# A two-layer hybrid step on one core: the attention stage's instruction order rewritten on every engine, and a second and third place for the output projection in PSUM

## The chip, the cores and the metric

The kernel runs on one core of a Trainium2 chip. The metric is the device time of one execution in microseconds (us), the median of three runs: 1716.8 us (1716.34 to 1719.81). Engines are named as in the profile: PE (matrix multiply) with its weight loads PEld, DVE (vector), ACT (activation), POOL (GpSimd), SP (the queue that issues the transfers).

## The reference, cut to what matters

Two layers act on 1024 prompt tokens and 64 sample tokens. Each layer projects the normed input, runs a gated recurrence (branch A), a top-k attention (branch B, 4 heads) and a differential attention (branch C, 4 heads with two softmax maps each), concatenates the three, projects with `w_out`, norms, and adds to the input. All of the change lies in the attention and output-projection part:

```python
def dsa_block(...):                                   # branch B
    s = einsum('bqhd,bqkhd->bqhk', q, k_sel) * (B_HEAD_DIM ** -0.5)
    p = softmax(where(valid, s, -inf))
    return einsum('bqhk,bqkhd->bqhd', p, v_sel)
def diff_block(...):                                  # branch C
    s = einsum('bqhid,bkhid->bhiqk', q, k) * (C_HALF ** -0.5)
    p = softmax(where(mask, s, -inf), axis=-1)
    attn = p[:, :, 0] - lam * p[:, :, 1]
    return rmsnorm(einsum('bhqk,bkhe->bqhe', attn, v), subln) * (1.0 - lam_init)
...
    mix = einsum('ble,ed->bld', concatenate([y_a, y_b, y_c], axis=-1), p['w_out'])
    x = x + rmsnorm(mix, p['norm_post'])
```

## The kernel before, in words

A layer has a front (input projections, index scores, top-k by bisection, recurrence), which the change doesn't touch, and then the **attention stage**. There are nine tiles of query tokens, taken in `ORDER` = 7, sample, 6, 0, 1, 2, 3, 4, 5; tile t < 8 has 128 tokens and sees 128(t+1) keys, the sample has 64 tokens and 1088 keys. `ATT` (L100) lists 70 **units**, one per tile, branch and head: first the four C heads, then the B heads of a tile (the sample's B heads are taken two at a time). "Wide" below means more than 512 keys (tiles 7, 6, 4, 5 and the sample), "narrow" at most 512 (tiles 0 to 3). A C unit of a prompt tile has two score maps, every other unit one.

A unit i goes through these steps, and each has one engine:
- `qk` (PE, L1663 to L1704): the scores of a map into one of two PSUM **slots**, used in turn; DVE takes the row maximum (`tensor_reduce`, L1454) and ACT the exponential (L1141), which frees the slot.
- `combine` (DVE, L575 to L597): the reciprocal of the sums (L585, L592, L593); in a prompt C unit also a factor (L595) and the difference of the two maps over the full width (L597). It signals `comb_ready`.
- `tr` (PE, L1717): transposes of up to four 128-key blocks into the one bank `tbank`; a copy to SBUF empties it (L570, by ACT in C units, by DVE in B units). A unit has one group of blocks (narrow), two (wide) or three (the sample). The first transpose waits for `comb_ready`, each group for the copy of the group before it.
- `pv` (PE, L1736): probabilities by values into the bank `obank`; `divide` (DVE, L613 to L627) scales it out.

After the last unit of a tile, POOL norms and gates the attention output (L918 to L928), `ytr` (PE, L1746) transposes it, ACT copies it (L1157), and the **output projection** `proj` (PE, L1775; L1770 for the sample) runs in 16 steps of two matmul rows each (8 steps for the sample) into `mixb`, PSUM banks 2 and 3. Then `square` (ACT, L1178) sums squares, POOL makes the factor (L937, L939), and `rows` (DVE, L1481; L1477 for the sample) scales `mixb` out and frees it; POOL adds the input (L946) and SP stores. Of the eight banks, even slots hold banks 0 to 2, odd slots 3 to 5, except that prompt tiles' odd slots begin at bank 4 (L497), which keeps banks 2 and 3 free for `mixb`.

The order is one list, `STEPS`, written by `schedule()` (L123). Every engine walks the same list in its own program and executes the steps that concern it, in that order and never out of order. Around unit i the list of before reads: first map's `qk` of unit i+1; for a wide unit then `rows`, the second `qk` of i+1, a projection step, `tr` i group 0, more projection steps, `pv` i-1, the other groups of `tr` i; for a narrow one a projection step, `pv` i-1, `rows`, the second `qk`, more projection steps, `tr` i. `QUOTA` says how many projection steps a unit of a tile gets, `hold` keeps the next tile's projection back for two units after a `square`, since there is one `mixb`. `ytr` of a tile comes after the third unit of the next tile (`YTR` = 2), before the next `qk`. DVE has no steps of its own for `combine` and `divide`: it does `combine(i-1)` ahead of the row maximum of unit i's first map (L1449), and `divide(i-1)` after the copy of `tr` i group 0 (L1463). ACT does a map's exponential at the place of its `qk`. When the units are over, the rest of tile 4's projection runs, then `square`, `rows`, `ytr` of tile 5, whose projection waits for that `rows`.

Of the kernel before, what the change touches and what calls it, by code (L numbers as in the profile page):

```python
# [6 lines left out]
P = 128  # L7
DM = 1024
KT = DM // P
NPR, NSA = 1024, 64  # L10
N = NPR + NSA
NT = 9
# [77 lines left out]
QUOTA = {0: 3, 1: 3, 2: 3, 3: 3, 4: 2, 5: 2, 6: 1}  # L90
YTR = 2
LAST_ROWS = [("tm", "cv", 3), ("tm", "cv", 4)]
# [29 lines left out]

def schedule():  # L123
# [5 lines left out]
    hold = [FIRST[ORDER.index(SAMPLE) + 1] + FIRST_PROJ]  # L129

    def qk(i):
        return [("qk", i, m) for m in range(maps_of(i))]

    def take(i, most):

        new = []
        while waiting and most and i >= hold[0]:
# [9 lines left out]
    steps += qk(0) + LAST_ROWS  # L147
    for i, (t, kind, h) in enumerate(units):
        nk = -(-width(t) // P)
        groups = [("tr", i, g) for g in range(-(-nk // 4))]  # L150
        nxt = qk(i + 1) if i + 1 < len(units) else []
        rows_now = [("rows", finish.pop(0))] if finish else []
        quota = QUOTA.get(t, 0)
        pv = [("pv", i - 1)] if i else []
        steps += nxt[:1]
# [4 lines left out]
        n = NTH[i]  # L160
        if i - FIRST[n] == YTR and n:
            steps.append(("ytr", n - 1))
            waiting += [(n - 1, q) for q in range(proj_steps(ORDER[n - 1]))]
    last = len(units)
    hold[0] = last
    steps.append(("pv", last - 1))
    steps += [("rows", n) for n in finish]
    while waiting:
        hold[0] = last
        new = take(last, 2 * KT)  # L170
        steps += new + ([("rows", new[-1][1])] if new[-1][0] == "square" else [])
    steps.append(("ytr", NT - 1))
# [74 lines left out]
TJOB = {k: n for n, k in enumerate([s for s in STEPS if s[0] in ("tr", "ytr")])}  # L247

# [5 lines left out]
def build(nc, x0, w_in, acst, gate_w, npost, w_out, ckT, kidxT, vcache,  # L254
# [7 lines left out]
    with ctx:  # L262
# [131 lines left out]
        mixb = ps[:, 2 * BANK:4 * BANK].rearrange("p (s b) -> p s b", s=2)  # L394
# [180 lines left out]
        def combine(dve, link, i, f):  # L575
# [8 lines left out]
            if kind == "B":  # L584
                vec.reciprocal(rr[0], d[0]).then_inc(comb_ready, 1)  # L585
                return
            if t == SAMPLE:
                link(vec.reciprocal(rr[0], d[0]))
                r1 = rr[0][NSA:P, :]
                vec.tensor_tensor(r1, r1, nlam[NSA:P, :], ALU.mult).then_inc(comb_ready, 1)  # L590
# [39 lines left out]
        for layer in range(DEPTH):  # L630
            x_from = y if layer else x0
            with nc.Block() as block:  # L632
# [317 lines left out]
                def _(act):  # L950
# [181 lines left out]
                    for s in STEPS:  # L1132
                        if s[0] == "qk":
# [7 lines left out]
                            ins = nc.scalar.activation(ex[2 * (i % 2) + m][0:r, 0:w], on_slot(s, w, r), ACT.Exp,  # L1141
# [727 lines left out]
```

## Time and profile before

| | |
|---|---|
| median of 3 runs | 1716.8 us |
| the profiled execution: its own time, its span | 1713.17 us, 1711.4 us |
| PE, DVE, ACT, POOL busy | 1579.6, 1130.6, 626.8, 425.3 us (92%, 66%, 37%, 25%) |
| attention stage, layer 1 and layer 2 | from 463 to 857 us, from 1320 to 1702 us of the span |
| mean granted PE clock over the span | 0.973 |

The profiled execution took 1.8 us more than its span and 3.6 us less than the median of the runs shown. A row of the timeline has the start, the length, the engine, the line of the kernel, the operation, output and inputs, the count of merged instructions, and in brackets the idle time of the engine before it with what ended it. A granted clock of 1.00 is TensorE's level of 2.4 GHz, 0.50 the level of 1.2 GHz; a stretch between the two spent part of its time at each.

### The profile page before, as it was taken

How to read it: one execution, taken by the hardware profiler on the slowest of the kernel's cores; microseconds unless marked ns; L12 is line 12 of the kernel's file. 1: busy time of each engine (PE TensorE's matmuls, PEld its weight loads, DVE VectorE, ACT ScalarE, POOL GpSimd, SP SyncE). 2: the span in 40 equal slices, each digit the busy share in tenths (PEclk: the TensorE clock that was granted, in tenths of full speed). 3: DMA queues.
4: the chain of work that ended last, by engine and by line, in shares of the span. 5: the costliest groups of instructions: out<-in, count | busy, mean ns of one | idle time of the engine just before them, and what ended most of it. 6: DMA issues, size and time to landing. Idle time of an engine off the chain costs nothing. (4 is left out here: it accounts for less than half of the span.)

```text
span 1711.4 us, 21022 instructions
## 1 busy us (share of the span) xinstructions
PE 1579.6 (92%) x7276; PEld 1083.2 (63%) x7298; DVE 1130.6 (66%) x2456; ACT 626.8 (37%) x1227; POOL 425.3 (25%) x540
## 2 busy tenths in 40 slices
PE   6999999999988889999859999999999888899996
PEld 3566566688876755567435665666888667555663
DVE  3478999948963655465134789999589646545550
ACT  2285520228143333333022756202280433333330
POOL 2001621520020344342120016205200213444411
PEclk9999999999998999999979999999999999999999
DMA  5100001321050311110151000013210503111101
GB/s 175 53 25 25 25 25 50 100 76 35 1 185 4 113 38 58 40 38 32 49 187 53 25 25 25 25 50 99 65 47 0 183 6 117 42 52 37 51 24 56
DMA packets 39177, 99.19 MB, mean 58 GB/s; under 512 B 8672, under 2 KB 27616, under 8 KB 34720
## 3 DMA queue, kind: packets, MB, share of 16 engines
q1 hardware_dynamic: 39072, 97.85, 17.3%
q8 instruction: 59, 0.97, 0.2%
q14 instruction: 46, 0.38, 0.1%
HBM read 66.84 MB, written 18.14 MB: 50 GB/s over the span
## 5 line engine op out<-in xcount | busy, mean ns | idle before, releaser
L1551 PE MATMUL ps<-r_xn,r_w 128*128 128x384 f32 (+1 forms) x1728 | 555.3, 473 | 12.3 <-DVE r_xn L1218 7.5
L1551 PEld LDWEIGHTS ps<-r_xn,r_w 128*128 128x128 f32 x1728 | 326.0, 191 | 195.7 <-issue 18.5
L1319 DVE TENSOR_SCALAR_CACHE_REDUCE r_ix<-r_sc,smi 128x768 bf16<-128x768 f32 (+6 forms) x380 | 342.0, 962 | 2.2
L1141 ACT ACTIVATE r_sc<-ps,sm 128x1024 f32<-128x1024 f32 (+8 forms) x204 | 155.7, 764 | 346.4 <-DVE sm L1454 339.2
L1454 DVE TENSOR_REDUCE sm<-ps 128x1 f32<-128x1024 f32 (+8 forms) x204 | 157.2, 784 | 121.8 <-PE ps L1699 52.1
L1627 PE MATMUL ps<-r_w,r_xn 128*128 128x256 f32 x1024 | 223.4, 380 | 0.0
L1627 PEld LDWEIGHTS ps<-r_w,r_xn 128*128 128x128 f32 x1024 | 193.9, 190 | 27.3 <-issue 1.0
L1736 PEld LDWEIGHTS ps<-r_vg,r_w 128*128 128x128 f32 (+1 forms) x1176 | 149.9, 194 | 52.9 <-issue 25.4
L1736 PE MATMUL ps<-r_vg,r_w 128*128 128x64 f32 (+1 forms) x1176 | 151.9, 274 | 6.3 <-DVE r_w L613 3.0
L1717 PE MATMUL ps<-ident,r_sc 128*128 128x128 f32 (+1 forms) x684 | 118.0, 282 | 39.1 <-ACT r_w L570 28.1
L1775 PE MATMUL ps<-r_xn,r_ag 128*128 128x512 f32 x256 | 137.5, 644 | 14.4 <-DVE r_res L1481 11.4
L1717 PEld LDWEIGHTS ps<-ident,r_sc 128*128 128x128 f32 (+1 forms) x684 | 83.7, 148 | 95.4 <-issue 46.8
L1775 PE MATMUL ps<-r_xn,r_vg 128*128 128x512 f32 x256 | 126.8, 604 | 0.1
L1281 DVE SCALAR_TENSOR_TENSOR r_sc<-r_vg,sm,r_sc 128x384 f32<-128x384 f32 (+6 forms) x98 | 97.8, 998 | 28.9 <-ACT r_vg L1056 23.4
L1056 ACT ACTIVATE r_vg<-ps 128x384 f32<-128x384 f32 (+6 forms) x112 | 88.4, 795 | 29.9 <-PE ps L1588 24.3
L570 DVE COPY r_w<-ps 128x512 f32<-128x512 f32 (+3 forms) x104 | 58.7, 565 | 60.3 <-PE ps L1717 59.3
L613 DVE TENSOR_SCALAR r_w<-ps,sm 128x64 f32<-128x64 f32 x128 | 35.7, 279 | 80.0 <-PE ps L1736 80.0
L1696 PE MATMUL ps<-kst_c,qc_hi 128*128 128x512 f32 (+3 forms) x192 | 79.4, 414 | 3.5 <-ACT r_sc L1141 2.0
L570 ACT COPY r_w<-ps 128x512 f32<-128x512 f32 (+3 forms) x112 | 55.0, 491 | 61.9 <-PE ps L1717 61.9
L1775 PEld LDWEIGHTS ps<-r_xn,r_ag 128*128 128x128 f32 x256 | 46.9, 208 | 41.4 <-issue 25.8
L783 POOL COPY sm<-r_ax 128x3 f32<-128x3 f32 x8 | 4.0, 501 | 271.3 <-ACT r_ax L995 271.3
L1588 PE MATMUL ps<-iks,iqs 128*128 128x384 f32 (+3 forms) x160 | 68.7, 500 | 1.5 <-ACT iqs L1038 1.5
(244 smaller groups left out, 2068.5 us busy)
## 6 DMA issues: line engine op xcount, KB each, us to landing
r_w<-w_in SPq DMA_DIRECT2D x28, 1024.0 KB, 4.9
r_xn<-w_out SPq DMA_DIRECT2D x2, 4096.0 KB, 13.5
y<-r_res SPq DMA_DIRECT2D x16, 512.0 KB, 2.9
r_vg<-x SPq DMA_DIRECT2D x8, 512.0 KB, 9.9
r_xn<-ckT SPq DMA_DIRECT2D x2, 2048.0 KB, 8.3
r_xn<-vcache SPq DMA_DIRECT2D x2, 2048.0 KB, 13.8
o_v<-r_vg SPq DMA_DIRECT2D x4, 1024.0 KB, 11.1
r_sc<-x SPq DMA_DIRECT2D x8, 512.0 KB, 4.9
```

Of the source, the lines that this page charges most:

```text
L570: ins = copy(pT[i % 2][:, k0:k1, 0:r], src[:, 0:k1 - k0, 0:r])
L1056: drains_x(nc.scalar.activation(dst, src, ACT.Relu, scale=scale), key)
L1141: ins = nc.scalar.activation(ex[2 * (i % 2) + m][0:r, 0:w], on_slot(s, w, r), ACT.Exp, bias=negm[0:r, c:c + 1], accum_out=den[0:r, c:c + 1])
L1281: ins = vec.scalar_tensor_tensor(sc[t][0:r, 0:w], src, iw[0:r, t, h:h + 1], sc[t][0:r, 0:w], ALU.mult, ALU.add)
L1319: ins = vec.tensor_scalar(unsel[t][0:rows(t), :], sc[t][0:rows(t), :], b, None, op, ALU.add, accum_out=cnt[0:rows(t), c:c + 1])
L1454: vec.tensor_reduce(negm[0:r, c:c + 1], on_slot(s, w, r), X, ALU.max, negate=True)\
L1551: ins = nc.tensor.matmul(on_ring(key, cn), w[:, k, P * s:P * (s + 1)], xnT[:, k, c0:c0 + cn], start=(k == 0), stop=(k == KT - 1))
L1627: ins = nc.tensor.matmul(on_ring(key)[:, BW * (t - t0):BW * (t - t0 + 1)], xnT[:, k, P * t:P * (t + 1)], w[:, k, :], start=(k == 0), stop= ...
L1696: ins = nc.tensor.matmul(out, q, kst[kind][:, h, c0:c0 + cn], start=(n2 == 0), stop=(n2 == 1 and not more))
L1717: ins = nc.tensor.transpose(tbank[0:kn, P * (k - 4 * g):P * (k - 4 * g) + r], ex[2 * (i % 2)][0:r, P * k:P * k + kn], ident[0:r, 0:r])
L1736: ins = nc.tensor.matmul(obank[0:r, 0:vals.shape[1]], pT[i % 2][0:kn, k, 0:r], vals, start=(k == 0), stop=(k == nk - 1))
L1775: ins = nc.tensor.matmul(mixb[:, half, :], yk, wo[:, k, BANK * half:BANK * (half + 1)], start=(k == 0), stop=(k == KT - 1))
```

## The change

- **Order on DVE and ACT.** `exp`, `comb` and `div` become steps of the list of their own, so that an exponential, a combine and a divide can stand apart from the `qk` or `tr` they were tied to. In wide prompt units the list now reads: first `qk` of i+1, its `exp`, `comb` i, `rows`, second `qk` of i+1, a projection step, `tr` i group 0, the second map's `exp`, projection steps, `pv` i-1, `div` i-1, the other groups. On DVE, `combine(i)` so comes behind the row maximum of unit i+1's first map. In narrow C units `comb` i stays ahead of it, in narrow B units it comes behind. In the sample, the exponential of unit i+1 comes after the copy of `tr` i group 0; PE's order there is as before. `qk2` splits the sample's `qk` at bank borders in the list, but both parts stand together.
- **comb_ready** is now signalled only by units with two maps; the transposes of other units wait for the exponential alone.
- **ytr** of a tile now comes after the next unit's `qk` and ahead of its exponential.
- **PSUM.** Odd slots of narrow tiles use bank 1, so banks 2 to 5 are free there: the projections of ORDER's places 1 and 3 (the sample, tile 0) go to banks 4 and 5, the last one (tile 5) to banks 0 and 1, all others to 2 and 3. A projection waits only for the last one in the same place.
- **Spread of the projection.** `QUOTA` of tiles 1 and 2 falls from 3 to 2; the hold of two units stays only where the next projection has the same place; `rows` comes at least one unit after its `square`. At the end, tile 5's `ytr` comes ahead of the last but one `rows`, and its projection no longer waits for that `rows`.

PE's work is the same in number and shape. The core of the diff:

```diff
-QUOTA = {0: 3, 1: 3, 2: 3, 3: 3, 4: 2, 5: 2, 6: 1}
+QUOTA = {0: 3, 1: 2, 2: 2, 3: 3, 4: 2, 5: 2, 6: 1}
+NARROW_MIX = (1, 3)
+NARROW_END = 7
+def mix_place(n):
+    return 1 if n in NARROW_MIX else 2 if n == NT - 1 else 0
+def same_place(n):
+    return [m for m in range(n) if mix_place(m) == mix_place(n)]
...
+        return [[("qk", i, m)] + ([("qk2", i, m)] if units[i][0] == SAMPLE else []) + [("exp", i, m)]
+                for m in range(maps_of(i))]
...
-                finish.append(n)
-                hold[0] = i + 2
+                late = 2 if mix_place(n + 1) == mix_place(n) else 1
+                finish.append((i + 1, n))
+                if late == 2:
+                    hold[0] = i + 2
...
+        div = [("div", i - 1)] if i else []
+        if i - FIRST[n] == YTR + 1 and n:
+            ytr = [("ytr", n - 1)]
+            waiting += [(n - 1, q) for q in range(proj_steps(ORDER[n - 1]))]
+        nxt = scores(i + 1)
+        one, two = (nxt + [[], []])[:2]
+        own = [("comb", i)]
+        plain = t == SAMPLE or kind == "B"
         if len(groups) == 1:
-            steps += take(i, 1) + pv + rows_now + nxt[1:] + take(i, quota - 1) + groups
+            head = one[:-1] + ytr + one[-1:] + own if plain else own + one[:-1] + ytr + one[-1:]
+            steps += head + take(i, 1) + pv + rows_now + two + take(i, quota - 1) + groups + div
+        elif t == SAMPLE:
+            steps += one[:-1] + ytr + own + rows_now + two[:-1]
+            steps += groups[:1] + one[-1:] + two[-1:] + pv + div + groups[1:]
         else:
-            steps += rows_now + nxt[1:] + take(i, 1) + groups[:1] + take(i, quota - 1) + pv + groups[1:]
+            steps += one[:-1] + ytr + one[-1:] + own + rows_now + two[:-1]
+            steps += take(i, 1) + groups[:1] + two[-1:] + take(i, quota - 1) + pv + div + groups[1:]
...
-        mixb = ps[:, 2 * BANK:4 * BANK].rearrange("p (s b) -> p s b", s=2)
+        banks = ps[:, :].rearrange("p (s b) -> p s b", b=BANK)
+        mixbs = [banks[:, 2:4, :], banks[:, 4:6, :], banks[:, 0:2, :]]
...
-                slot = slot[:, BANK:]
+                slot = slot[:, BANK:] if width(ATT[key[1]][0]) > BANK else ps[0:r, BANK:2 * BANK]
...
-                            if m == 0 and i >= 1:
-                                combine(dve, link, i - 1, first[i - 1])
...
+                        elif s[0] == "comb":
+                            combine(dve, link, s[1], first[s[1]])
+                        elif s[0] == "div":
                             divide(dve, s[1], link)
...
-                            if g == 0:
-                                pe.wait_ge(comb_ready, i + 1)
+                            if g == 0 and COMBINED[i]:
+                                pe.wait_ge(comb_ready, COMBINED[i])
+                            elif g == 0:
+                                wait_drained(pe, ("qk", i, 0))
```

## Rows read from the trace of the kernel before

**Rows 1.** Windows, the attention stages: busy time by engine, then granted clock.

```profile
463.00:857.00 394.00, 354.64 (x1845) 238.81 (x1856) 199.81 (x493) 129.48 (x299) 115.00 (x175) 0.95 0.18 60
1320.00:1702.00 382.00, 344.44 (x1845) 233.67 (x1856) 198.34 (x492) 129.15 (x298) 114.17 (x173) 0.98 0.19 62
```

**Rows 2.** PE's waits, layer 2, narrow tiles: total us, times, longest.

```profile
PE ps L1775 <- DVE r_res L1481: 2.7, 2, 2.2
PE ps L1746 <- ACT r_w L570: 2.1, 4, 0.7
PE ps L1736 <- DVE r_w L613: 1.5, 4, 0.4
PE ps L1770 <- DVE r_res L1481: 1.4, 1, 1.4
PE ps L1775 <- DVE r_res L1477: 1.3, 1, 1.3
PE ps L1736 <- ACT r_w L570: 1.0, 1, 1.0
```

**Rows 3.** PE's waits, layer 2, the sample (1376 to 1418.5 us).

```profile
PE ps L1717 <- ACT r_w L570: 5.5, 8, 1.0
PE ps L1717 <- DVE r_w L570: 2.2, 2, 1.2
```

**Rows 4.** PE's waits, layer 2, tile 7's C units (1320 to 1357 us).

```profile
PE ps L1717 <- ACT r_w L570: 5.2, 4, 2.7
```

**Rows 5.** PE's waits, layer 2, tile 6's C units (1418.5 to 1440 us).

```profile
PE ps L1717 <- ACT r_w L570: 2.9, 3, 1.3
PE ps L1746 <- ACT r_w L570: 0.6, 1, 0.6
```

**Rows 6.** Windows, layer 2, the C units of tiles 4 and 5: busy time.

```profile
1592.00:1614.00 22.00, 20.94 (x120) 14.69 (x120) 13.15 (x33) 9.77 (x24) 6.07 (x9) 1.00 0.05 13
1624.00:1650.00 26.00, 25.01 (x145) 18.31 (x145) 17.05 (x38) 11.28 (x24) 2.19 (x3) 1.00 0.16 52
```

**Rows 7.** Timeline, layer 2, around the transposes of tile 7's third C unit.

```profile
1343.67 0.16 DVE L592 RECIPROCAL sm<-sm 128x1 f32<-128x1 f32 x1
...
1344.23 1.28 DVE L597 SCALAR_TENSOR_TENSOR r_sc<-r_sc,sm 128x1024 f32<-128x1024 f32 x1
...
1344.31 0.48 PE L1696 MATMUL ps<-kst_c,qc_hi 128*128 128x512 f32 x1
...
1345.33 0.23 PE L1702 MATMUL ps<-chunk,diagm 128*128 128x128 bf16 x1
...
1345.37 0.48 PE L1696 MATMUL ps<-kst_c,qc_hi 128*128 128x512 f32 x1
...
1345.60 2.36 DVE L1454 TENSOR_REDUCE sm<-ps 128x1 f32<-128x1024 f32 x2
...
1346.45 0.61 PE L1717 MATMUL ps<-ident,r_sc 128*128 128x128 f32 x4
```

**Rows 8.** Groups by shape, DVE, layer 2: busy us, mean ns; idle before.

```profile
L1454 DVE TENSOR_REDUCE sm<-ps 128x1 f32<-128x896 f32 x12 | 12.8, 1086 | 5.2 <-PE ps L1699 3.5 <-PE ps L1702 1.7
L1454 DVE TENSOR_REDUCE sm<-ps 128x1 f32<-128x768 f32 x12 | 11.1, 951 | 2.3 <-PE ps L1699 2.1 <-PE ps L1702 0.2
...
L597 DVE SCALAR_TENSOR_TENSOR r_sc<-r_sc,sm 128x896 f32<-128x896 f32 x4 | 4.7, 1174 | 0.1
...
L597 DVE SCALAR_TENSOR_TENSOR r_sc<-r_sc,sm 128x768 f32<-128x768 f32 x4 | 4.1, 1034 | 0.1
```

**Rows 9.** Timeline, PE: tile 5's projection in layer 1, its first four steps.

```profile
836.81 6.58 PE L1775 MATMUL ps<-r_xn,r_ag 128*128 128x512 f32 x8 [3.07 <-DVE r_res L1481]
```

**Rows 10.** The chain that ended last, layer 2: the same projection, whole.

```profile
1687.26 14.02 PE ps L1775 x32
```

**Rows 11.** Timeline, ACT, layer 2: the copy behind the last transposes.

```profile
1684.81 0.59 ACT L1157 ACTIVATE r_vg<-ps 128x512 f32<-128x512 f32 x1
```

**Rows 12.** A window in layer 1's narrow tiles: busy time, then granted clock.

```profile
697.00:703.00 6.00, 6.00 (x15) 3.31 (x14) 1.35 (x3) 1.55 (x4) 3.81 (x5) 0.53 0.56 188
```

More of the change, by code:

```diff
@@ L129, in schedule, with scores @@
     hold = [FIRST[ORDER.index(SAMPLE) + 1] + FIRST_PROJ]
-    def qk(i):
-        return [("qk", i, m) for m in range(maps_of(i))]
+    begun = [0]
+    def scores(i):
+        if not begun[0] <= i < len(units):
+            return []
+        begun[0] = i + 1
+        return [[("qk", i, m)] + ([("qk2", i, m)] if units[i][0] == SAMPLE else []) + [("exp", i, m)]
+                for m in range(maps_of(i))]
     def take(i, most):
@@ L142, in take @@
                 new.append(("square", n))
-                finish.append(n)
-                hold[0] = i + 2
+                late = 2 if mix_place(n + 1) == mix_place(n) else 1
+                finish.append((i + 1, n))
+                if late == 2:
+                    hold[0] = i + 2
         return new
-    steps += qk(0) + LAST_ROWS
+    steps += sum(scores(0), []) + LAST_ROWS
     for i, (t, kind, h) in enumerate(units):
@@ L150, in schedule @@
         groups = [("tr", i, g) for g in range(-(-nk // 4))]
-        nxt = qk(i + 1) if i + 1 < len(units) else []
-        rows_now = [("rows", finish.pop(0))] if finish else []
+        rows_now = [("rows", finish.pop(0)[1])] if finish and finish[0][0] <= i else []
         quota = QUOTA.get(t, 0)
         pv = [("pv", i - 1)] if i else []
-        steps += nxt[:1]
-        if len(groups) == 1:
-            steps += take(i, 1) + pv + rows_now + nxt[1:] + take(i, quota - 1) + groups
-        else:
-            steps += rows_now + nxt[1:] + take(i, 1) + groups[:1] + take(i, quota - 1) + pv + groups[1:]
[L160 to L163, printed above, removed]
+        div = [("div", i - 1)] if i else []
+        n = NTH[i]
+        ytr = []
+        if i - FIRST[n] == YTR + 1 and n:
[5 more added lines that the diff above has]
+        plain = t == SAMPLE or kind == "B"
+        if len(groups) == 1:
+            head = one[:-1] + ytr + one[-1:] + own if plain else own + one[:-1] + ytr + one[-1:]
[3 more added lines that the diff above has]
+            steps += groups[:1] + one[-1:] + two[-1:] + pv + div + groups[1:]
+        else:
+            steps += one[:-1] + ytr + one[-1:] + own + rows_now + two[:-1]
+            steps += take(i, 1) + groups[:1] + two[-1:] + take(i, quota - 1) + pv + div + groups[1:]
     last = len(units)
     hold[0] = last
-    steps.append(("pv", last - 1))
-    steps += [("rows", n) for n in finish]
+    steps += [("pv", last - 1), ("div", last - 1)]
     while waiting:
         hold[0] = last
-        new = take(last, 2 * KT)
-        steps += new + ([("rows", new[-1][1])] if new[-1][0] == "square" else [])
-    steps.append(("ytr", NT - 1))
+        steps += take(last, 2 * KT)
+    steps += [("ytr", NT - 1)] + [("rows", n) for _, n in finish]
     waiting += [(NT - 1, q) for q in range(proj_steps(ORDER[-1]))]
@@ L247 @@
 TJOB = {k: n for n, k in enumerate([s for s in STEPS if s[0] in ("tr", "ytr")])}
+COMBINED = [0 if maps_of(i) == 1 else sum(maps_of(k) == 2 for k in range(i + 1)) for i in range(len(ATT))]
 def groups_of(i):
@@ L1457, in _ @@
                         elif s[0] == "tr":
-                            i, g = s[1], s[2]
-                            if g == 0 and i == len(ATT) - 1:
-                                combine(dve, link, i, first[i])
-                            if ATT[i][1] == "B":
-                                evac_pT(dve, vec.tensor_copy, i, g)
-                            if g == 0 and i >= 1:
-                                divide(dve, i - 1, link)
-                        elif s[0] == "pv" and s[1] == len(ATT) - 1:
+                            if ATT[s[1]][1] == "B":
+                                evac_pT(dve, vec.tensor_copy, s[1], s[2])
+                        elif s[0] == "comb":
+                            combine(dve, link, s[1], first[s[1]])
+                        elif s[0] == "div":
                             divide(dve, s[1], link)
```

48 lines of the change are left out of this document (32 added, 16 removed).

## The prediction

> **What bounds the kernel now.** First the windows of the two attention stages [rows 1], the only part that the change touches: 394 and 382 us, in which PE works 354.6 and 344.4. PE is the bound, and what the stage can give is PE's idle time, 39.4 and 37.6 us, and its low clock: mean grants of 0.95 and 0.98 mean that up to 5% of 394 = 19.7 us and 2% of 382 = 7.6 us of full-speed time were lost. Then PE's waits, stage by stage in layer 2, where the reader sees three kinds. In the narrow tiles [rows 2] PE waits for `rows` before a projection (2.7, 1.4 and 1.3: 5.4 us), for the last copy before `ytr` (2.1) and, in units without projection steps, for `divide` or a copy (1.5, 1.0): 10.0 us in 13 waits. In the sample [rows 3] and the C units of tile 7 [rows 4] and tile 6 [rows 5] it waits for ACT's copy between two groups of transposes. The C units of tiles 4 and 5 have only 22.00 - 20.94 = 1.06 and 26.00 - 25.01 = 0.99 us idle [rows 6]. Last, the timeline of one wide C unit [rows 7] shows why there is no stall at the first transposes there: `combine` starts at 1343.67, before PE begins the next unit's scores at 1344.31, and PE goes from those straight to the transposes at 1346.45.
>
> A wait in that view counts from the modelled end of the last matmul; without a wait the next would start about 0.2 us earlier (1345.33 + 0.23 = 1345.56 against the successor at 1345.37 [rows 7]). So each wait that goes brings its length and some 0.2 us.
>
> **What it takes away.** All sums are per layer.
> - *Narrow tiles.* The sample's and tile 0's projections have banks of their own, and steps are spread, so a projection seldom meets an undone `rows`; `ytr` finds `tbank` empty because 0.5 to 1 us of scores stand ahead of it; nearly every unit has steps to cover the copies. 10.0 + 13 x 0.2 = 12.6 us; I leave 1.6 for the one unit without steps (before tile 3's `rows` ends) and for the projection still behind a `rows` in the same place: **-11.0**. The cover for DVE's in-order wait at `rows` is now three projection steps at 14.02 / 16 = 0.88 us [rows 10], which hide 2.6 us; the longest such wait was 2.2 [rows 2].
> - *The sample.* The copy no longer stands behind the next exponential. Of the eight waits on ACT (5.5 us) [rows 3] the four for the third group, one copy each, stay; I take 2.8 us and, with `ytr`, five times 0.2 and 0.3: **-4.0**. The two on DVE (2.2) stay.
> - *The end.* Tile 5's projection waited 3.07 us for `rows` [rows 9]; now it needs only the copy behind `ytr`, which ACT ended at 1684.81 + 0.59 = 1685.40 [rows 11] against a start at 1687.26 [rows 10]: **-1.8**.
> - *Clock.* After the wait at the end in layer 1 four steps took 6.58 us [rows 9], in layer 2 a quarter of 14.02 = 3.5 [rows 10]: -3.1 in layer 1 alone. In the narrow tiles of layer 1 the grant fell to 0.53 over 6 us of full work after the longest `rows` wait [rows 12], worth 2.8, and I count two such falls less well filled: -5.0; in layer 2 a third of its 7.6: -2.5.
>
> Quota, hold and the `tr` wait on the exponential alone move no work of PE: the same 1845 matmul rows. The POOL chain, the pads of the queries and SP's transfers keep their places to within one unit; they are covered by whole tiles of work, and if not, are in the first rival.
>
> **What it adds.** In wide prompt C units DVE must now take the maximum of the next unit's first map *before* `combine`, and PE's first transposes need that combine. The loop is: first scores end, maximum, combine, transposes, `pv`, transposes, next scores. From the point where the second map's scores start to the transposes it takes, at 1024 keys, half of 2.36 + (1344.23 - 1343.67 + 1.28) = 1.18 + 1.84, plus 0.3 of ends and semaphores (1345.60 - 1345.37 [rows 7] and one more hop) = 3.3 us. PE covers 1346.45 - 1345.37 = 1.1 of it. Queued behind the combine on DVE is the second map's maximum, for which ACT's second exponential waits.
> - Tile 7, four units: 3 x 2.2, and 3.3 in the last, whose successor has one map, and 0.6 for the very first second group = 10.5; it replaces 5.2 + 4 x 0.2 = 6.0 [rows 4]: **+4.5**.
> - Tile 6: 1.09 + 1.17 + 0.56 + 0.3 = 3.1 [rows 8], cover 0.9, and in the last unit `ytr` and a step, 1.3: 3 x 2.2 + 1.8 = 8.4, for 3.5 + 0.8 [rows 5]: **+4.1**.
> - Tile 5: 0.95 + 1.03 + 0.56 + 0.3 = 2.8 [rows 8]; cover 0.85 of scores and a step of 0.88, at the last unit 1.3: 3 x 1.1 + 1.5 = 4.8, for 0.99 + 0.6 [rows 6]: **+3.2**. Tile 4, by its 640 keys an estimate of 2.4 for the lag and 0.75 for the scores: 3 x 0.8 + 1.1 = 3.5, for 1.06 + 0.6: **+1.8**.
>
> Sum +13.6. No row shows PE's clock with these stalls. Below: -1, since matmuls slowed beside the DVE chain cost nothing. Above: with all 16 units at the lower level, a step costs 6.58 / 4 - 0.88 = 0.8 more [rows 9, 10]; with scores and transposes in the loop I estimate 1.0 per unit in tiles 7 and 6 and 1.9 in 5 and 4, 23 us. Layer 2's stage kept 0.98 with 5.2 us of waits in tile 7 alone [rows 1, 4], so the nearest rows speak for the low end: I take +1.5.
>
> **Sum.** Layer 1: -11.0 - 4.0 - 1.8 - 3.1 - 5.0 + 13.6 + 1.5 = -9.8. Layer 2: -11.0 - 4.0 - 1.8 - 2.5 + 13.6 + 1.5 = -4.2. Together -14: the profiled execution, 1713.2 by its own time, would take 1699. The median of the runs shown is 3.6 us above it, and I give the forecast on that scale: 1716.8 - 14 = **1703 us**, 0.8% less.
>
> **The clock rule.** What the rows show: the same 3.07 us wait was followed by 6.58 us for four steps in layer 1 and by 3.5 in layer 2 [rows 9, 10], so the fall depends on more than the wait. The Trainium skill, "TensorE: Matmul & The Clock Gate", section "What's actually happening", says that the slow state is the default, that activity lifts it, and that where the change comes depends on a phase that runs free of the kernel. By that rule the stalls added to wide tiles work against the change as the removed ones work for it, and shifting everything redraws all falls; the trace agrees with the second part. With none of the clock terms' 3.1 + 5.0 + 2.5 = 10.6 us the sum would be 1714; the whole of what the rule can do here is the third rival.
>
> **The rivals.**
> 1. *The `rows` waits only move* (12%). DVE works in order; where it stands at `rows` for POOL's factor, the next copy and maximum stand too, and PE then stops at `pv` or `tr` instead of at the projection. For it: the tiles' gating stands ahead of that factor in POOL's queue. Against: three steps of cover. Half of 11.0 in both layers and half of the narrow clock gain would be lost: 11.0 + 7.5 / 2 = 15 us more, 1718.
> 2. *The wide loop hardly costs* (15%). If exponentials that start 1.8 us earlier shorten the rest (copies, slots), or PE falls less often in the sample too, half of +13.6 goes, twice: 1703 - 14 = 1689. Against: every link of the loop is a true dependence.
> 3. *Slower: the clock in the wide tiles* (11%). The stalls of 1 to 2 us in 16 consecutive-in-kind units pull PE to the lower level there. At 23 us per layer for all of them and 1.5 already counted, it decides from (14 + 3) us upward, that is from (17 + 3) / 46 = 45% of these units; at 60%, 0.6 x 46 - 3 = 25 us more, 1728. For it: in tile 7 a unit stalls 2.2 us again and again, as long as the wait ahead of the fall of [rows 12]. Against: layer 2 kept a mean of 0.98 with 5.2 us of waits in tile 7 alone [rows 1, 4].
>
> **How the numbers follow.** The forecast has 62%: 1703, its own range 1694 to 1712 from the 1.6 us left over in the narrow tiles, the clock terms (10.6 of the gain, taken wrong by half) and the -1 to some +4 per layer in the wide ones. To leave out no more than 2 in 10, the range reaches to rival 2's end and just over rival 1: 1688 to 1719. Differences within 0.2%, 3.4 us, are about what a measurement of this kernel can't tell from no change. Faster by more: 60 of the 62, all 15 of rival 2, 2 of rival 1: 77%. Same: 2, 8 of rival 1: 11% with one from rival 3. Slower: the rest, 12%.
>
> **What would show it.** In the changed profile: PE's waits for `rows` (L1481, L1477 of before) before projections gone in the narrow tiles, and at the end a wait of about 1.3 us for ACT; no wait for `r_w` copies in the first group of the sample's C units; and as a new entry, the first transposes waiting for DVE's difference of maps (L597) 16 times a layer, twelve times for 0.8 to 2.2 us and four times (before each first B unit) for 1.1 to 3.3, 27 us a layer in all (10.5 + 8.4 + 4.8 + 3.5). Wrong would be: few waits on that combine (then the wide term falls), as many waits as before in the narrow tiles on `divide` or copies (rival 1), or a mean grant in the stages under 0.93 (rival 3).

## The result and the profile after

| | before | after |
|---|---|---|
| median (lowest to highest) | 1716.35 us (1706.64 to 1725.67, 20 runs) | 1731.45 us (1719.96 to 1737.95, 20 runs) |
| ratio to before, 95% interval | | 1.0093 (1.0076 to 1.0109) |
| span of the profiled execution | 1711.4 us | 1735.6 us |
| mean granted PE clock | 0.973 | 0.962 |

The change costs 15 us, 0.9%, where 14 us less were forecast; 1731 lies above the top of the range, 1719. Among the runs of the changed kernel the time follows the grant: the fastest, 1719.96 us, had a mean of 0.974, the slowest, 1737.95 us, one of 0.961.

The page of the changed kernel: busy time, and the clock in 40 slices of the span.

```profile
PE 1592.8 (92%) x7298; PEld 1095.1 (63%) x7298; DVE 1131.8 (65%) x2456; ACT 630.6 (36%) x1227; POOL 427.8 (25%) x540
...
PEclk9999999999979899999979999999999698999999
```

The dips to 7 and 6 in the 12th and 32nd slice are the first tiles of the two attention stages, those to 8 two slices on are tile 6. The 21st, the front of layer 2, had its 7 before the change too. The windows of these stages, the counterpart of [rows 1] (busy time by engine, then the grant):

```profile
465.00:857.00 392.00, 350.95 (x1854) 239.76 (x1855) 200.13 (x492) 130.34 (x297) 115.73 (x173) 0.95 0.18 61
1329.00:1724.00 395.00, 353.33 (x1854) 241.73 (x1855) 199.42 (x492) 130.16 (x296) 115.35 (x173) 0.94 0.18 60
```

Layer 1 kept its 0.95, layer 2 fell from 0.98 to 0.94, and PE is *busy* 9 us longer there on the same matmuls: a slower clock shows as busy time, not as waits. To place this, both traces are cut where PE begins the first transposes of each tile in the timeline (tile 7's stage begins at its first scores, and the last one ends with the last projection matmul; the cuts are good to some 0.5 us, the same way in both traces). "Low" is the time in the stage at a grant of 0.50.

| stage, us (low) | layer 1 before | after | layer 2 before | after |
|---|---|---|---|---|
| tile 7, C units | 36.2 (3.4) | 48.2 (20.5) | 36.3 (3.4) | 49.8 (26.1) |
| sample | 46.6 (10.2) | 41.2 (0) | 45.3 (6.8) | 42.5 (3.4) |
| tile 6, C units | 24.8 (6.8) | 27.9 (10.2) | 22.6 (0) | 28.4 (10.2) |
| tiles 0 to 3 | 135.6 (13.6) | 129.6 (6.9) | 132.2 (6.8) | 129.0 (3.4) |
| tiles 4 and 5, C and B | 89.9 (0) | 92.6 (0) | 89.9 (0) | 92.6 (0) |
| after the last `ytr` | 20.0 (6.8) | 15.3 (0) | 17.1 (0) | 15.3 (0) |
| whole stage | 389.6 (41.0) | 392.1 (37.5) | 380.1 (17.1) | 395.4 (44.4) |

(The table leaves out the B units of tiles 7 and 6, which moved by 1.1 at most. Tiles 0 to 3 hold three projection steps more after the change, 66 and the sample's 8 in place of 63 and 8, and tiles 4 and 5 three fewer; at 0.88 us a step this is 2.6 us a layer that only moved from one row to the other. The two fronts, before the attention stages, took 1.6 and 4.3 us more, though the change edits nothing there.)

**The new waits.** PE's waits in layer 2: in order the C units of tile 7, tile 6, tile 4 and tile 5. Columns: total us, times, longest.

```profile
PE ps L1757 <- DVE r_sc L628: 8.8, 4, 3.2
...
PE ps L1757 <- DVE r_sc L628: 6.0, 3, 2.0
...
PE ps L1757 <- DVE r_sc L628: 3.5, 4, 1.1
...
PE ps L1757 <- DVE r_sc L628: 4.1, 4, 1.3
```

L628 is the difference of maps (L597 before). Where PE waited for ACT's copies before [rows 4, 5] it now waits for the combine, at the sizes forecast: tile 7's four are 2.10, 1.84, 1.64 and 3.17 us (2.2 three times and 3.3 had been taken). The window of tile 6 ends ahead of the fourth of its waits, 1.1 us.

**What a unit costs at the low clock.** Timeline of PE, tile 7's second and third C units in layer 2 (the same place as [rows 7]):

```profile
1351.91 0.63 PE L1757 MATMUL ps<-ident,r_sc 128*128 128x128 f32 x4 [1.84 <-DVE r_sc L628]
1352.38 3.30 PE L1776 MATMUL ps<-r_vg,r_w 128*128 128x64 f32 x16
1355.47 1.06 PE L1757 MATMUL ps<-ident,r_sc 128*128 128x128 f32 x4
1356.18 0.78 PE L1733 MATMUL ps<-kst_c,qc_hi 128*128 128x512 f32 x1
...
1361.61 0.63 PE L1757 MATMUL ps<-ident,r_sc 128*128 128x128 f32 x4 [1.64 <-DVE r_sc L628]
```

From one unit's first transposes to the next's it is 9.7 us. `pv` takes 3.30 us, and the second group of transposes 1.06 against 0.63 for the first, which still ran at a grant of 1.00 (2.4 GHz); the scores come after those. The stall on DVE and the low clock stand in the same unit, unit after unit.

**What went away.** PE's waits of layer 2 in the sample, the narrow tiles (t0 to t3), and after the last `ytr`:

```profile
PE ps L1757 <- ACT r_w L601: 2.7, 4, 0.7
PE ps L1757 <- DVE r_w L601: 2.3, 2, 1.2
...
PE ps L1776 <- DVE r_w L644: 2.5, 2, 1.5
PE ps L1733 <- ACT r_sc L1172: 2.0, 2, 1.6
PE ps L1757 <- DVE r_sc L628: 1.7, 1, 1.7
...
PE ps L1819 <- ACT r_vg L1188: 1.3, 1, 1.3
```

In the sample four of the eight waits on ACT [rows 3] are left. Every wait for `rows` ahead of a projection [rows 2] is gone, and so is that at the end, with 1.3 us for the copy in its place as forecast. But the narrow tiles have a new cluster, 2.5 + 2.0 + 1.7. It lies in one spot, at the border of tiles 0 and 1. The timeline of that spot, all engines:

```profile
1507.63 2.35 POOL L977 TENSOR_TENSOR r_res<-r_res,r_sc 128x1024 f32<-128x1024 f32 x1
1510.00 0.35 SPq L766 DMA_DIRECT2D y<-r_res  x1
1513.09 0.59 ACT L1203 ACTIVATE r_res<-ps 64x512 f32<-64x512 f32 x1 [4.90 <-DMA y<-r_res]
...
1514.91 0.46 ACT L1172 ACTIVATE r_sc<-ps,sm 128x256 f32<-128x256 f32 x1
...
1515.51 0.38 PE L1733 MATMUL ps<-kst_c,qc_hi 128*128 128x256 f32 x1 [1.58 <-ACT r_sc L1172]
...
1516.27 0.74 DVE L1506 SCALAR_TENSOR_TENSOR r_res<-ps,sm,r_ix 64x512 f32<-64x512 f32 x1 [4.86 <-POOL sm L970]
...
1518.54 0.41 PE L1776 MATMUL ps<-r_vg,r_w 128*128 128x64 f32 x2 [1.54 <-DVE r_w L644]
...
1519.13 2.33 POOL L977 TENSOR_TENSOR r_res<-r_res,r_sc 64x1024 f32<-64x1024 f32 x1
1519.30 2.45 DVE L628 SCALAR_TENSOR_TENSOR r_sc<-r_sc,sm 128x256 f32<-128x256 f32 x1
...
1521.89 0.41 PE L1757 MATMUL ps<-ident,r_sc 128*128 128x128 f32 x2 [1.67 <-DVE r_sc L628]
```

The sample's square (L1203) begins with a copy into the staging rows from which tile 7's result is still being stored (L766). It stands 4.90 us on ACT for that store, with the next exponential behind it; POOL's factor (L970) comes late by as much, DVE stands 4.86 us at the sample's `rows` (L1506) with a maximum, a copy and a division behind it, and PE stops twice for it. The third stop, 1.67 us, has another cause, the long L628 at 1519.30 (last section).

### The profile page after: what moved, and what is told of

It is laid out like the page before. It is cut to its first block and busy times, and to the rows that moved or that the text cites. A ratio compares the mean times of both kernels' runs of the same rounds, so it can differ in the third digit from the quotient of the medians.

```text
span 1735.6 us, 21040 instructions
## 1 busy us (share of the span) xinstructions
PE 1592.8 (92%) x7298; PEld 1095.1 (63%) x7298; DVE 1131.8 (65%) x2456; ACT 630.6 (36%) x1227; POOL 427.8 (25%) x540
## 3 DMA queue, kind: packets, MB, share of 16 engines
q1 hardware_dynamic: 39072, 97.85, 17.1%
## 5 line engine op out<-in xcount | busy, mean ns | idle before, releaser
L1580 PE MATMUL ps<-r_xn,r_w 128*128 128x384 f32 (+1 forms) x1728 | 561.0, 477 | 13.7 <-DVE r_xn L1250 8.3
L1656 PEld LDWEIGHTS ps<-r_w,r_xn 128*128 128x128 f32 x1024 | 193.9, 190 | 27.3 <-issue 1.0
L1776 PEld LDWEIGHTS ps<-r_vg,r_w 128*128 128x128 f32 (+1 forms) x1176 | 159.4, 204 | 56.9 <-issue 23.5
L1757 PE MATMUL ps<-ident,r_sc 128*128 128x128 f32 (+1 forms) x684 | 122.5, 291 | 67.6 <-DVE r_sc L628 49.4
L1776 PE MATMUL ps<-r_vg,r_w 128*128 128x64 f32 (+1 forms) x1176 | 160.9, 285 | 7.5 <-DVE r_w L644 5.0
L1819 PE MATMUL ps<-r_xn,r_ag 128*128 128x512 f32 x256 | 131.2, 610 | 2.7 <-ACT r_vg L1188 2.7
L1819 PE MATMUL ps<-r_xn,r_vg 128*128 128x512 f32 x256 | 130.3, 613 | 0.0
L1313 DVE SCALAR_TENSOR_TENSOR r_sc<-r_vg,sm,r_sc 128x384 f32<-128x384 f32 (+6 forms) x98 | 97.8, 998 | 30.3 <-ACT r_vg L1087 24.7
L1136 ACT ACTIVATE r_ix<-r_sc,smi 128x896 bf16<-128x896 f32 (+2 forms) x60 | 67.1, 1120 | 6.6 <-DVE smi L1392 6.4
```

The costliest lines, as they stand in the source:

```text
L1313: ins = vec.scalar_tensor_tensor(sc[t][0:r, 0:w], src, iw[0:r, t, h:h + 1], sc[t][0:r, 0:w], ALU.mult, ALU.add)
L1580: ins = nc.tensor.matmul(on_ring(key, cn), w[:, k, P * s:P * (s + 1)], xnT[:, k, c0:c0 + cn], start=(k == 0), stop=(k == KT - 1))
L1656: ins = nc.tensor.matmul(on_ring(key)[:, BW * (t - t0):BW * (t - t0 + 1)], xnT[:, k, P * t:P * (t + 1)], w[:, k, :], start=(k == 0), stop= ...
L1757: ins = nc.tensor.transpose(tbank[0:kn, P * (k - 4 * g):P * (k - 4 * g) + r], ex[2 * (i % 2)][0:r, P * k:P * k + kn], ident[0:r, 0:r])
L1776: ins = nc.tensor.matmul(obank[0:r, 0:vals.shape[1]], pT[i % 2][0:kn, k, 0:r], vals, start=(k == 0), stop=(k == nk - 1))
L1819: ins = nc.tensor.matmul(mixb[:, half, :], yk, wo[:, k, BANK * half:BANK * (half + 1)], start=(k == 0), stop=(k == KT - 1))
```

## The experiments

Eleven kernels, in three groups; `before` ran beside each group, with medians of 1718.1, 1716.7 and 1718.4 us. Stage times are cut as above.

### Group 1: the order of the combine, the clock, the square

**comb_first**: the changed kernel, with the combine ahead of the next unit's first maximum again in the wide C units.

```diff
-            steps += one[:-1] + ytr + one[-1:] + own + rows_now + two[:-1]
+            if kind == "C":
+                steps += own + one[:-1] + ytr + one[-1:] + rows_now + two[:-1]
+            else:
+                steps += one[:-1] + ytr + one[-1:] + own + rows_now + two[:-1]
```

Expected: 

> The changed kernel with one step moved back: in wide prompt C units combine(i) stands ahead of the next unit's first row maximum on DVE again. Theory (the combine behind the maximum stalls PE, and the stalls pull its clock down): the 16 waits of PE on the difference of maps per layer go from 25 us (profile of after, both kinds of size) to under 3, tile 7's C stretch falls from 48 and 50 us to 37 or less, tile 6's from 28 to 23, tiles 4 and 5 lose 2 us each; in all 20 to 24 us per layer with the clock, so 1731 - 44 = about 1690, under the kernel before. Rival (the stretch is slow for the exponential that was put behind the first copy, or the clock falls there for another reason): under 10 us of gain, tile 7's C stretch stays over 43.

Measured: 1677.18 us (1675.31 to 1679.85), ratio to before 0.9772 (0.974 to 0.9804), mean clock 0.984. It is 54 us below the changed kernel, where 41 to 44 had been expected, and 39 below before.

**before_behind**: the kernel before, with the same order turned the other way, alone.

```diff
+                            behind = i >= 1 and maps_of(i - 1) == 2 and width(ATT[i - 1][0]) > BANK
-                            if m == 0 and i >= 1:
+                            if m == 0 and i >= 1 and not behind:
                                 combine(dve, link, i - 1, first[i - 1])
...
+                            if m == 0 and behind:
+                                combine(dve, link, i - 1, first[i - 1])
```

Expected: 

> The kernel before with one thing of the change: in wide prompt C units the combine comes behind the next unit's first row maximum on DVE; exponentials, PSUM places and the spread of the projection stay as before. Theory: PE's first transposes wait for the combine 16 times a layer; tile 7's C stretch grows from 36 to 46 to 50 us, tile 6's from 23 to 28, tiles 4 and 5 by 2 to 3 each, so 1716 + 2 x 19 = about 1750 (1740 to 1760). Rival (the loss comes of the combination with the moved exponential or with the narrow tiles' new shape): under 15 us slower.

Measured: 1775.47 us (1771.53 to 1778.57), ratio 1.034 (1.0309 to 1.0372), slower than the range expected: tile 7's C units took 52 us, 27.3 of them low, in each layer. With the kernel before, the changed one and comb_first this closes a square: the combine's place costs 57 us on the kernel before and 54 on the changed one, and all else in the change gains 41 (1718 to 1677) or 44 (1775 to 1731). The parts add to within 3 us. The terms other than the wide loop had promised 24.9 + 19.3 = 44 over both layers (the section on the prediction asks how far they came true one by one); the place of the combine had been put at 2 x (13.6 + 1.5) = 30.

**filler**: the changed kernel, with bf16 matmuls of 128x512 ahead of the first transposes of tile 7's second, third and fourth C units (9, 9 and 14 of them). They write to a bank that nobody reads then; nothing of the work is left out.

```diff
+                            if g == 0 and NTH[i] == 0 and ATT[i][1] == "C" and 1 <= i:
...
+                                for _ in range(9 if i < 3 else 14):
+                                    nc.tensor.matmul(ps[:, 2 * BANK:3 * BANK], diagm[:, :], unsel[7][:, 0:BANK],
+                                                     start=True, stop=True)
```

Expected: 

> The changed kernel with matmuls added that compute nothing: 9 bf16 128x512 matmuls into the unused third bank ahead of the first transposes of tile 7's second and third C unit, 14 ahead of the fourth's, to fill PE's stall on the combine (2.2 and 3.2 us). Theory (a stall of 2.2 us by the chain, and the rest of tile 7's +12 by the clock that the stall pulls down): with the stall filled the clock stays up in tile 7, its C stretch falls from 48 to 50 us to 41 to 43 (7.0 us a unit by the chain), 10 to 15 us less in all, about 1718. Rival (the clock falls for what the transposes and value products themselves are, not for the idle time): the stretch stays at 48 or more, the time at 1731 or above.

Measured: 1718.82 us (1714.17 to 1720.82), ratio 1.0009 (0.9988 to 1.003), which is 12.6 us below the changed kernel's 1731.45, for work that does nothing. The windows of tile 7's C units, in both layers, first of the changed kernel:

```profile
465.00:513.00 48.00, 38.62 (x194) 31.11 (x195) 24.01 (x37) 17.62 (x31) 4.37 (x8) 0.79 0.46 162
1329.00:1379.00 50.00, 40.57 (x196) 32.19 (x197) 23.98 (x37) 17.45 (x30) 4.27 (x8) 0.74 0.43 155
```

of filler:

```profile
465.00:506.00 41.00, 37.62 (x223) 27.38 (x227) 24.07 (x38) 17.71 (x31) 4.38 (x8) 0.96 0.54 190
1321.00:1361.00 40.00, 36.92 (x228) 26.59 (x232) 23.88 (x38) 17.32 (x30) 4.38 (x8) 1.00 0.54 195
```

and of comb_first:

```profile
466.00:501.00 35.00, 30.05 (x194) 23.65 (x195) 24.02 (x37) 16.82 (x31) 3.42 (x8) 1.00 0.56 197
1299.00:1334.00 35.00, 30.31 (x199) 23.82 (x199) 23.78 (x38) 16.66 (x30) 3.42 (x8) 1.00 0.57 204
```

The changed kernel's matmuls took 38.6 and 40.6 us here, the same ones in comb_first 30.1 and 30.3. With the stalls filled, the stage falls to 41.0 and 39.7 us; in layer 2 the grant is 1.00 throughout. DVE's loop is as it was, so 39.7 against comb_first's 34.8 is the stalls alone, 4.9 us (at most: a filler may have run past the end of its gap), and 49.8 against 39.7 is the clock, 10.1. The stalls pull the clock down, and not the other way. The Trainium skill, "TensorE: Matmul & The Clock Gate", section "What's actually happening", says that the slow state is the default and activity lifts it; by that rule matmuls without use should pay here, and they do.

**square_late**: the changed kernel, with the sample's square and `rows` one unit later.

```diff
-                new.append(("square", n))
...
-                finish.append((i + 1, n))
+                if ORDER[n] == SAMPLE:
+                    later.append((i + 1, n))
+                    finish.append((i + 2, n))
```

Expected: 

> The changed kernel with the sample's square one unit later and its rows one unit later, in ACT's, POOL's and DVE's order; PE's order is the same. Theory: in the changed kernel ACT stood 4.9 us at that square for the store of tile 7's rows to leave the result buffer, with the next exponential behind it, and DVE 4.9 us at the rows, and PE's waits of 1.6, 1.5 and 1.7 us after it come from there; so 3 to 5 us per layer come back, 1731 - 8 = about 1723, and stretch t0 plus t1 falls by 3 to 5. Rival (POOL's chain sets it, gating before the factor): no change, or the waits move one unit on.

Measured: 1719.45 us (1704.55 to 1728.22), ratio 0.9999 (0.9966 to 1.0032), 12 us below the changed kernel. Tiles 0 to 3 took 124.4 and 124.3 us, 5.2 and 4.7 less, all of it in tile 0's stage (34.1 to 28.6). The runs spread over 24 us; that the clock in the wide tiles, which differs from run to run, makes this spread is likely, but not shown.

### Group 2: the two edits together, tile 7 alone, the exponential, the banks

**both**: comb_first and square_late together.

Expected: 

> The changed kernel with two edits: the combine back ahead of the next unit's first maximum in the wide C units, and the sample's square and rows one unit later. If the two act apart from each other: comb_first measured 1677, and the narrow tiles t0 to t3 of square_late were 4 to 5 us a layer shorter than comb_first's (124.3 against 128.1 in both layers), so 1677 - 8 = 1669. Theory: ScalarE's square stood for the store of tile 7's rows with the next exponential behind it, which is independent of the wide C order. Rival (the gain of square_late is only a redrawn clock): 1674 to 1679, with the narrow tiles at 128.

Measured: 1667.15 us (1662.43 to 1669.52), ratio to before 0.9703 (0.9669 to 0.9738), clock 0.985. This beats both kernels of the case, by 3.0% and 3.7%. The whole attention stages are 358.3 and 358.7 us, without any time at the low clock. The square no longer waits; the timeline of ACT at the same spot:

```profile
1454.29 0.47 ACT L1184 ACTIVATE r_sc<-ps,sm 128x256 f32<-128x256 f32 x1 [0.67 <-DVE sm L1497]
...
1454.88 0.59 ACT L1215 ACTIVATE r_res<-ps 64x512 f32<-64x512 f32 x1
```

The exponential now stands ahead of it, and the store has landed.

**first_t7**: the combine back ahead in tile 7 alone (`if kind == "C" and t == 7:` in comb_first's edit).

Expected: 

> The changed kernel with the combine back ahead of the next unit's first maximum in tile 7's C units alone (8 of the 32 wide C units of both layers). Theory (the clock is lost where the stalls are longest): tile 7's C units give back 48.2 - 34.8 + 49.8 - 34.8 = 28 us of the 54 that all the wide units give, total about 1731 - 28 = 1703 (1698 to 1708), which is the time I had predicted; tile 6 keeps its low clock (28 us a layer's C units). Rival (it is the mere number of stalls, evenly worth): a quarter to a third of 54, 1713 to 1718.

Measured: 1705.67 us (1701.9 to 1709.83), ratio 0.9937. Of the 54 us the 8 units of tile 7, a quarter of the wide C units, hold 26, which speaks for the theory. Tile 6's C units still pay the low clock; their window in layer 2:

```profile
1406.00:1433.00 27.00, 22.85 (x125) 17.82 (x125) 12.90 (x31) 10.95 (x21) 6.02 (x9) 0.81 0.42 166
```

against this one in comb_first:

```profile
1392.00:1414.00 22.00, 18.35 (x126) 14.88 (x126) 15.41 (x32) 11.37 (x23) 5.37 (x9) 1.00 0.52 203
```

Tiles 4 and 5 cost 7.2 us a layer (tile 3's last unit included), against 7.6 of waits, and no clock: their stalls, at most 1.3 us and with projection steps around them, left the grant at 1.00 in both layers of the changed kernel and of before_behind.

**exp_back**: comb_first, with the second map's exponential (and the sample's) ahead of the copy of the first group again.

```diff
-            steps += groups[:1] + one[-1:] + two[-1:] + pv + div + groups[1:]
+            steps += one[-1:] + two[-1:] + groups[:1] + pv + div + groups[1:]
...
-            steps += take(i, 1) + groups[:1] + two[-1:] + take(i, quota - 1) + pv + div + groups[1:]
+            steps += two[-1:] + take(i, 1) + groups[:1] + take(i, quota - 1) + pv + div + groups[1:]
```

Expected: 

> comb_first with the second map's exponential (and the sample's) back ahead of the copy of the first group of transposes: the part of the change that its author names, undone alone. Theory: in the sample five ACT waits of about 0.5 us come back (4.0 a layer by my prediction, 5 to 7 by the stages measured, with clock), in tiles 7 and 6 the waits of 5.2 and 2.9 us in the C units come back, with cover of the clock unknown: 1677 + 2 x (5 + 4) = 1695 (1688 to 1702). Rival (the copy is hidden either way): 1677 to 1680.

Measured: 1693.55 us (1689.54 to 1694.89), 16 us above comb_first. PE's waits on ACT's copies in layer 2, sample and tile 6's C units, of exp_back and then of comb_first:

```profile
PE ps L1760 <- ACT r_w L604: 7.9, 10, 1.3
```

```profile
PE ps L1760 <- ACT r_w L604: 3.5, 6, 0.7
```

4.4 us of waits in one layer, where -4.0 had been forecast for the sample. The total was met, its place only in part: the sample took 5.3 and 0.9 us more than in comb_first; tile 7's C units took 36.4 us (with 3.4 low) and 34.9, hardly more than comb_first's 34.8, so copies cost nothing there; the rest of the 16 us is 1.6 a layer in the C units of tiles 4 and 5, and clock (20.5 and 6.8 us low in the two stages, against 6.8 in each).

**one_place**: comb_first, with all projections but the last in banks 2 and 3 (`mix_place` gives 0 for them).

Expected: 

> comb_first with the narrow tiles' projections all in banks 2 and 3 again (the last tile's stays apart), so that each projection must wait until the one before it has been read; the quota and all else as in the changed kernel. Theory: the waits for the rows before projections come back in the narrow tiles, partly covered since a hold of two units is planned for each: +2 to +4 us a layer, 1677 + 6 = 1683 (1679 to 1688). Rival (the places do nothing, the hold alone does it): within 1677 to 1679.

Measured: 1705.31 us (1699.57 to 1706.68), 28 us above comb_first, far above what either theory gave. With one place a projection is held back for two units, and with the changed quota of two steps in tiles 1 and 2 it doesn't catch up: 29 of a layer's 136 steps come in tile 5's B units and right behind them in place of 17. They are missed earlier, it seems: PE's waits in the narrow tiles have 3.7 us on ACT's copies ahead of `pv` and 1.4 and 1.2 for `rows`.

### Group 3: the quota and the transposes of the rows

**one_place_q**: one_place with the old quota, `QUOTA = {0: 3, 1: 3, 2: 3, 3: 3, ...}`.

Expected: 

> one_place with the projection quotas of the kernel before (three steps a unit in tiles 1 and 2): the places and the spread undone together, everything else as in comb_first. In one_place twelve of a layer's steps had slid behind the last unit, where they cover nothing; here two or so do. Theory (most of one_place's 28 us came from steps that had left the narrow units and so covered nothing): the time falls back to 1677 + 2 x 5 = 1687 (1682 to 1694). Rival (waiting for one pair of banks is what costs): 1700 or more.

Measured: 1691.74 us (1688.45 to 1697.92): 13.6 of the 28 us go with the quota, and so with the steps that had slid to the end. The other 14.6 are what places and spread are worth together. Tiles 0 to 3, counting a step as 0.88 us, are 10 us longer than comb_first's in layer 1 and 5 in layer 2, with 20.5 and 6.8 us at the low clock there against 6.8 and 3.4.

**both_q**: the version both with the old quota, the places kept.

Expected: 

> The version both with the projection quotas of the kernel before (three a unit in tiles 1 and 2 in place of two), the places kept. The steps come sooner, so later units have none to cover their copies: same or slower, 1667 to 1675. Rival (spreading was not needed): 1664 to 1667.

Measured: 1707.93 us (1701.01 to 1711.51), 41 us above both. I had missed this altogether. With three steps a unit the early tiles use up the supply (24, 24, 16 and 16 steps in tiles 0 to 3, in place of 23, 16, 17 and 18), and six units have none, the second and third of tiles 2, 3 and 4; in both only two units of tiles 0 to 4 have none. Tile 3's stage in layer 2 takes 44.7 us against 35.1, with 13.7 at the low clock. PE's waits there, of both_q:

```profile
PE ps L1788 <- ACT r_w L613: 2.8, 2, 1.5
PE ps L1745 <- ACT r_sc L1184: 1.1, 3, 0.5
PE ps L1831 <- ACT r_vg L1200: 0.8, 1, 0.8
```

They are 4.7 us, and the stage lost 9.6, with two steps fewer in it; over the whole attention stages both_q has 20.5 and 27.3 us at the low clock, where both has none. So much of the 41 us is clock again. The two edits belong together: one place goes with the old quota (1692 against 1705 us), places of their own with the new one (1667 against 1708, this pair with the sample's late square). Either alone is worse than none.

**ytr_back**: the version both, with the transposes of the finished rows at the end of the unit again, behind its last group.

```diff
-        if i - FIRST[n] == YTR + 1 and n:
-            ytr = [("ytr", n - 1)]
...
+        if i - FIRST[n] == YTR and n:
+            steps.append(("ytr", n - 1))
```

Expected: 

> The version both with the transposes of the finished tile's rows back at the end of the unit, behind the unit's last group, in place of behind the next unit's scores. My prediction gave this step 2.1 us a layer in the narrow tiles and 0.3 in the sample: 1667 + 5 = 1672 (1669 to 1676). Rival (the wait for the last copy only moves to the next group of transposes): within 1666 to 1668.

Measured: 1671.83 us (1670.43 to 1676.16; four runs), 4.7 above both. PE's waits in the narrow tiles of layer 2 have the old entry back, with the very numbers of [rows 2]:

```profile
PE ps L1798 <- ACT r_w L613: 2.1, 4, 0.7
```

## Why the prediction was wrong

**Where it was right.** The sixteen waits on the combine were foreseen in place and nearly in length: 8.8 us in tile 7 for 10.5, 7.1 in tile 6 for 8.4, 7.6 in tiles 4 and 5 for 8.3. Filler prices the loop in tile 7 without its clock at 39.7 - 36.3 = +3.4 us in layer 2, for the +4.5 forecast (before's 36.3 holds a low stretch of 3.4). The `ytr` term (2.1 in the narrow tiles and 0.3 in the sample, twice) measured 4.7. The sample, at -4.0, gave 5.4 and 2.8 us in the changed kernel, its low time (10.2 and 3.4 us less) included. The end gave 1.8 in layer 2 for 1.8, and 4.7 in layer 1 for 1.8 + 3.1.

**Luck.** That everything beside the combine's place came to 41 to 44 us, for 44, is partly luck. In comb_first the narrow tiles gave 7.5 + 2.6 and 4.1 + 2.6 = 16.8 us (their three steps more counted off) for 16.0 + 13.5 = 29.5. The 12.7 us missing were made up by the sample (11.3 for 8.0) and by tiles 7, 6, 4 and 5 (7.5), for which no such term stood.

**The step that failed** is the clock in the wide loop, taken at +1.5 us a layer. In tile 7 alone it measured 10.1 in layer 2 and some 8.5 in layer 1 (48.2 - 41.0, and 1.3 for the low stretch that filler's own stage has). Two things were wrong in it.
- *The choice between the bounds.* I took the low end because layer 2 had kept 0.98 with 5.2 us of waits in tile 7 [rows 1, 4]. Those 5.2 us were four waits of which one was 2.7; the change made them 8.8 in four, each unit with one, and the low time in tile 7 went from 3.4 to 20.5 and 26.1 us. It does not grow in proportion, and a mean over a stage of 382 us could not show it. The row that should have been weighed was the clock in the window of tile 7's units alone, which already had a low stretch in both layers.
- *The price of a unit.* I had 1.0 us for a unit at the low level, worked out from projection steps (0.8 each), scores and transposes, and left `pv` out. `pv` is sixteen matmul rows, 1.90 us at the high level (comb_first) and 3.52 at the low (the changed kernel's fourth unit), so a unit pays for it too: (49.8 - 39.7) / 4 = 2.5 us. The rows, first of comb_first, then of the changed kernel:

```profile
1317.66 1.90 PE L1779 MATMUL ps<-r_vg,r_w 128*128 128x64 f32 x16
```

```profile
1372.40 3.52 PE L1776 MATMUL ps<-r_vg,r_w 128*128 128x64 f32 x16
```

So the third rival is what happened by its mechanism: low clock in tiles 7 and 6, 8 of a layer's 16 wide units, just past the share from which it decides (20/46 = 43%; the prediction has 45%). That its 1728 us lie so near the 1731 measured is luck: it had 60% of the units at 1.0 to 1.9 us each, tile 7's paid 2.5, and over a third of the miss lies in the narrow tiles. Its sign, a mean grant under 0.93, did not appear (0.95 and 0.94), since a stage's mean hides a low loop. The argument against it was the same misread row, and it had 11% where the sum gave the first case 62%.

**The second step that failed** is -11.0 for the narrow tiles, with 5.0 and 2.5 for their clock: 29.5 us in both layers, of which 14.4 came (6.0 + 2.6 and 3.2 + 2.6). The sample's square is 5.2 and 4.7 of the missing 15.1 (square_late). The sentence that POOL's chain and SP's transfers "keep their places to within one unit" was used to set their cost to nothing. With banks of its own the sample's projection came earlier than the store of tile 7's rows could finish, and the wait for that store sits on ACT ahead of the next exponential. It is the first rival's mechanism (DVE stands at `rows` for POOL's factor, and PE stops behind it, here at the next scores and at `pv`), in one place a layer and set off by a DMA.

The other 5 us are mainly waits that stayed: even square_late has 4.3 us of them in seven waits in layer 2's narrow tiles, where 1.6 us had been left.

**The sum again**, stage by stage, both layers together, from the two profiled executions. They are 24.2 us apart, the medians 15: the changed kernel's lay 6 us above its median and that of before 3 below. So the table explains 38 us, where the miss by the medians is 28.5.

| us | forecast | measured | miss |
|---|---|---|---|
| tile 7, C units | +9.0 | +25.5 | 16.5 |
| tiles 0 to 3 (the moved steps counted off) | -29.5 | -14.4 | 15.1 |
| tile 6, C units | +8.2 | +8.9 | 0.7 |
| tiles 4 and 5 (the moved steps counted on) | +10.0 | +10.6 | 0.6 |
| sample | -8.0 | -8.2 | -0.2 |
| after the last `ytr` | -6.7 | -6.5 | 0.2 |
| clock in the wide loop | +3.0 | in the rows above | -3.0 |
| B units of tiles 7 and 6, fronts | 0 | +7.8 | 7.8 |

Tile 6 only looks well forecast: its loop is +1.7 a layer in place of +4.1 (28.4 us with 10.2 low in the changed kernel's layer 2, 26.8 with 6.8 in square_late, 25.6 with 3.4 in filler, so 0.4 for each us low and 24.3 without, on before's 22.6), and the clock made up for it. Each row is the difference of single profiles. The fronts, +1.6 and +4.3 us, stay open; no run tells them from chance.

## What to carry to other kernels

Price an added stall twice: its own length, and the clock of everything PE does in that loop, every matmul group counted, at the low level; a mean grant over a long stage says nothing of a loop in which each pass stalls. Where a wait can't be removed, fill it: here matmuls without use paid, and projection steps spread so that hardly a unit is without one were worth 41 us, clock included. And when a step is moved earlier, look for the slowest thing it waits for on an in-order engine, a store included, and for what is queued behind that wait.

## What was not expected of the hardware

- **A DVE instruction that lasts as long as POOL's.** In the timeline of the border above, L628 on 128x256 elements took 2.45 us beside POOL's L977 of 2.33 us; its neighbour four microseconds later took this, beside no POOL work of that kind:

```profile
1523.83 0.48 DVE L628 SCALAR_TENSOR_TENSOR r_sc<-r_sc,sm 128x256 f32<-128x256 f32 x1
```

  The kernel before has the pair as well:

```profile
1491.90 2.34 POOL L946 TENSOR_TENSOR r_res<-r_res,r_sc 64x1024 f32<-64x1024 f32 x1
...
1492.40 2.13 DVE L597 SCALAR_TENSOR_TENSOR r_sc<-r_sc,sm 128x256 f32<-128x256 f32 x1
```

  The thirteen kept traces together say more. In them 64 DVE instructions with two inputs from SBUF overlapped with this POOL operation, and each ended a fixed time after it: 0.28 us in 26 of 26 at 128x256, 0.41 in 6 of 6 at 128x384, 0.08 in 32 of 32 at 128x64 (those last 0.23 us otherwise, and 1.43 to 1.99 here). The 472 other DVE instructions beside it (copies, scalings, maxima, reciprocals, with one tensor input) kept their usual length to within 9%. The Trainium skill, "GPSIMD Engine Reference", section "Specifications", says that GpSimd's access to SBUF is shared with VectorE and contends with DVE instructions that have two SBUF inputs; the traces agree, and the DVE instruction stands until the POOL one is over. PE waited 1.67 us for it in the changed kernel, and 0.3 us in all for L597 in the narrow tiles of the one before (layer 2).
- **A large price for a small change in the stalls.** Tile 7's C units in layer 2 took 36.3 us with one low stretch and 49.8 with 26.1 us low, while PE's waits there grew by 3.6 us only (5.2 to 8.8).
- **The spread of the runs.** The changed kernel and square_late spread by 18 and 24 us over their runs, comb_first and both, whose wide C units were never low in the profile, by 5 and 7, and so did before_behind (7), whose tile 7 was low for 27.3 of 52 us in both layers.
